# Sample attention's ScalarE and VectorE chains issued inside their own tick instead of behind the next main step

## What is computed

```python
def stick_breaking_attention(q, kc, vc, q_pos, bias):
    z = jnp.einsum('bqhd,bkhd->bhqk', q, kc) * (HEAD_DIM ** -0.5) + bias
    valid = jnp.arange(kc.shape[1])[None, :] < q_pos[:, None]
    log_beta = jnp.where(valid, jax.nn.log_sigmoid(z), -jnp.inf)
    log_keep = jnp.where(valid, jax.nn.log_sigmoid(-z), 0.0)
    later = lax.cumsum(log_keep, axis=3, reverse=True) - log_keep
    a = jnp.exp(log_beta + later)
    return jnp.einsum('bhqk,bkhd->bqhd', a, vc)
```

## Time and profile before

| | |
|---|---|
| median of 3 runs | 2498.41 us (2497.21 to 2503.57) |
| the profiled execution | 2500.48 us, of which span 2498.8 us |
| PE busy | 2340.1 us, 94% |
| DVE busy | 1191.4 us, 48% |
| ACT busy | 929.4 us, 37% |
| POOL busy | 142.2 us, 6% |
| PE waiting for `sa_kt` copies of ACT ahead of L2508, layer 0's mixers | 8.7 us in 5 waits |
| PE waiting for L1587 ahead of L1646, layer 0's mixers | 1.3 us in 2 waits |

### The profile page before, as it was taken

One profiled execution on the slowest core, in us unless ns is written; L12 is line 12 of the kernel. 1 busy time (PEld: TensorE's weight loads), 2 busy tenths in 40 slices (PEclk: granted clock), 3 DMA queues, 4 the chain that ended last, 5 costly groups with the idle time before them and its releaser, 6 DMA issues. The chain is left out here.

```text
span 2498.8 us, 44904 instructions
## 1 busy us (share of the span) xinstructions
PE 2340.1 (94%) x17622; PEld 2087.6 (84%) x17622; DVE 1191.4 (48%) x2080; ACT 929.4 (37%) x1671; POOL 142.2 (6%) x195
## 2 busy tenths in 40 slices
PE   7999999989988899999999999999798888999997
PEld 7999998766656599999899999987565566999996
DVE  6343273245566566342463434622656565643425
ACT  5222242223425554222352323321333365532333
POOL 0000010011222000000000000100112200000000
PEclk8999999989989799999999999999898897999998
DMA  5233333145756443233333233421558645333333
GB/s 141 68 84 84 102 112 125 51 126 165 228 163 184 144 144 88 67 90 84 96 86 84 78 91 102 129 91 34 185 176 227 195 128 178 85 85 84 82 102 91
DMA packets 384957, 290.97 MB, mean 116 GB/s; under 512 B 51808, under 2 KB 368392, under 8 KB 384272
## 3 DMA queue, kind: packets, MB, share of 16 engines
q1 hardware_dynamic: 368128, 234.08, 33.3%
q0 software_dynamic: 16128, 54.54, 7.1%
q10 hardware_dynamic: 528, 0.02, 0.0%
HBM read 274.99 MB, written 13.58 MB: 115 GB/s over the span
## 5 line engine op out<-in xcount | busy, mean ns | idle before, releaser
L218 PE MATMUL ps<-h_hi,w_hi 128*128 128x288 f32 x2400 | 719.1, 300 | 24.2 <-PEq L174 17.3
L219 PE MATMUL ps<-h_lo,w_hi 128*128 128x288 f32 x2400 | 711.2, 296 | 0.0
L220 PE MATMUL ps<-h_hi,w_lo 128*128 128x288 f32 x2400 | 710.6, 296 | 0.0
L242 DVE TENSOR_TENSOR w_lo<-w_raw,w_hi 128x2048 fp32r<-128x2048 f32 x145 | 332.3, 2291 | 341.2 <-ACT w_hi L236 341.1
L218 PEld LDWEIGHTS ps<-h_hi,w_hi 128*128 128x128 f32 x2400 | 453.1, 189 | 30.3 <-issue 25.2
L219 PEld LDWEIGHTS ps<-h_lo,w_hi 128*128 128x128 f32 x2400 | 453.3, 189 | 1.0
L220 PEld LDWEIGHTS ps<-h_hi,w_lo 128*128 128x128 f32 x2400 | 453.1, 189 | 0.0
L236 ACT ACTIVATE w_hi<-w_raw 128x2048 fp32r<-128x2048 f32 x145 | 276.7, 1908 | 163.9 <-PE ps L220 159.6
L218 PE MATMUL ps<-f_a_hi,w_hi 128*128 128x288 f32 x1024 | 302.7, 296 | 0.0
L220 PE MATMUL ps<-f_a_hi,w_lo 128*128 128x288 f32 x1024 | 301.6, 295 | 0.0
L219 PE MATMUL ps<-f_a_lo,w_hi 128*128 128x288 f32 x1024 | 301.5, 294 | 0.0
(11 more groups left out here) (345 smaller groups left out, 3167.9 us busy)
## 6 DMA issues: line engine op xcount, KB each, us to landing
w_raw<-in_w_ffn_in SPq DMA_DIRECT2D x132, 512.0 KB, 5.2
w_raw<-in_w_ffn_out SPq DMA_DIRECT2D x80, 512.0 KB, 4.9
sa_vn<-in_cache_sb_v SPq DMA_DIRECT2D x256, 128.0 KB
w_raw<-in_w_in SPq DMA_DIRECT2D x52, 512.0 KB, 4.6
sa_vn<-in_cache_win_v SPq DMA_DIRECT2D x96, 128.0 KB
w_raw<-in_w_out SPq DMA_DIRECT2D x24, 512.0 KB, 6.5
sa_kn_early<-in_cache_win_k POOLq DMA_DIRECT2D x72, 128.0 KB, 3.8
sa_vn<-in_cache_win_v SPq DMA_DIRECT2D x16, 512.0 KB
```

The costliest lines, as they stand in the source:

```text
L218: pe.matmul(out, stat_hi, mov_hi, start=start, stop=False, skip_group_check=True)
L219: pe.matmul(out, stat_hi, mov_lo, start=False, stop=False, skip_group_check=True)
L220: return pe.matmul(out, stat_lo, mov_hi, start=False, stop=stop, skip_group_check=True)
L242: dve.tensor_tensor(E["w_lo"][:, slot], E["w_raw"][:, slot], E["w_hi"][:, slot].bitcast(F32), ALU.subtract).then_inc(S["w_lo"], 1)
```

## The change

The content of `scalar_behind` and `vector_behind` moves into the tick's own functions, and `weave` loses its deferred call. ACT's tick is now: key copy; window exponential; the exponential of the chunk due one tick ago; the three-instruction ACT chain of the chunk due now; and only then the copy of turned weights and the gathered output copy. DVE's tick is: key copy; the DVE chain of the chunk due one tick ago; `take`; window reduce; weight copy; `rows`. No instruction is added or removed, no wait changes, and PE, SP and POOL are issued as before. Weights are still turned in tick T+3.

```diff
     def scalar_tick(act, t):
         if t < U:
             copy_keys_a(act, t)
-        for m in G["turn_at"].get(t, ()):
-            if m % 2 == 0:
-                copy_weights_a(act, chunks[m])
-        if t - 1 in G["ends"]:
...
-    def scalar_behind(act, t):
         for q in rows_at(t, 1):
             act.wait_ge(S["negated"], q["row"] + 1)
...
             act.activation(f_of(c), f_of(c), ACT.Exp, scale=-1.0).then_inc(S["exp_done"], 1)
             act.wait_ge(S["exp_done"], s + 1)
             act.activation(f_of(c), f_of(c), ACT.Ln, bias=1.0).then_inc(S["ln_done"], 1)
+        for m in G["turn_at"].get(t, ()):
+            if m % 2 == 0:
+                copy_weights_a(act, chunks[m])
+        if t - 1 in G["ends"]:
...
             spread_queries(dve, True)
         if t < U:
             copy_keys_b(dve, t)
+        for c in weighed_at(t, 1):
+            s, w = c["stick"], c["width"]
+            dve.wait_ge(S["ln_done"], s + 1)
+            dve.scalar_tensor_tensor(f_of(c), z_of(c), 0.0, f_of(c), ALU.max, ALU.add).then_inc(S["f_done"], 1)
...
+            dve.wait_ge(S["sum_done"], s + 1)
+            dve.tensor_tensor(z_of(c), z_of(c), f_of(c), ALU.subtract).then_inc(S["scanned"], 1)
         for c in chunks:
             if c["tick"] == t:
                 take(dve, c)
+        for q in rows_at(t, 0):
+            dve.wait_ge(S["z_ready"], q["chunk0"] + q["chunks"])
+            dve.tensor_reduce(mx[:, q["g"]:q["g"] + 1], zw[:, q["g"]], AX.X, ALU.max).then_inc(S["maxed"], 1)
...
         for m in G["turn_at"].get(t, ()):
             if m % 2 == 1:
                 copy_weights_b(dve, chunks[m])
-
-    def vector_behind(dve, t):
         if t in G["ends"]:
             p = G["ends"][t]
             q = passes[p]
...
-    def weave(eng, name, behind=None):
+    def weave(eng, name):
         mains = {tag: p[name](eng) for tag, p in parts.items()}
-        done, left = 0, None
+        done = 0
         for tag, upto in zip(ORDER, plan):
             next(mains[tag])
-            if left is not None:
-                behind(eng, left)
-                left = None
             while done < upto:
-                if left is not None:
-                    behind(eng, left)
                 side[name](eng, done)
-                left = done if behind else None
                 done += 1
```

More of the change, by code:

```diff
@@ L2664, in scalar_behind @@
             act.activation(f_of(c), f_of(c), ACT.Ln, bias=1.0).then_inc(S["ln_done"], 1)
+        for m in G["turn_at"].get(t, ()):
+            if m % 2 == 0:
+                copy_weights_a(act, chunks[m])
+        if t - 1 in G["ends"]:
+            p = G["ends"][t - 1]
+            q = passes[p]
+            chunk, at = (4 if q["window"] else 6), SEQ + SG * DEC_SEQ * q["g"]
+            e = ev_a["g", p]
+            act.wait_ge(S["turned_a"], e + 1)
+            act.activation(M["mixT"][:, chunk:chunk + 2, at:at + SG * DEC_SEQ],
+                           ps[:, TURN_A[e % len(TURN_A)], 0:64].rearrange("p (k t) -> p k t", k=2),
+                           ACT.Copy).then_inc(S["free_a"], 1)
     def spread_queries(dve, window):
@@ L2725, in vector_tick @@
             copy_keys_b(dve, t)
+        for c in weighed_at(t, 1):
+            s, w = c["stick"], c["width"]
+            dve.wait_ge(S["ln_done"], s + 1)
+            dve.scalar_tensor_tensor(f_of(c), z_of(c), 0.0, f_of(c), ALU.max, ALU.add).then_inc(S["f_done"], 1)
+            dve.wait_ge(S["f_done"], s + 1)
+            carried = 0.0 if c["first"] else f[:, (s - 1) % Z_SLOTS, 0:1]
+            dve.tensor_tensor_scan(f_of(c)[:, ::-1], one[:, 0:1].to_broadcast([P, w]), f_of(c)[:, ::-1], carried,
+                                   ALU.mult, ALU.add).then_inc(S["sum_done"], 1)
+            dve.wait_ge(S["sum_done"], s + 1)
+            dve.tensor_tensor(z_of(c), z_of(c), f_of(c), ALU.subtract).then_inc(S["scanned"], 1)
         for c in chunks:
@@ L2749, in vector_behind @@
                 dve.tensor_tensor(rows[:], ps[:, OUT_BANK, 0:W4], head_cols[:], ALU.mult).then_inc(S["rows_ready"], 1)
[L2750 to L2765, removed]
     sticks = [c for c in chunks if not c["window"]]
@@ L2772, in sample_attention @@
     return dict(S=S, zw=zw, spent=spent, ticks=G["ticks"], early_sync=early_sync, early_gpsimd=early_gpsimd,
-                keys=[landed(False, U - SLOTS + x) for x in range(SLOTS)], sync=sync_tick, gpsimd=gpsimd_tick, tensor=tensor_tick, scalar=scalar_tick, vector=vector_tick,
-                scalar_behind=scalar_behind, vector_behind=vector_behind)
+                keys=[landed(False, U - SLOTS + x) for x in range(SLOTS)], sync=sync_tick, gpsimd=gpsimd_tick, tensor=tensor_tick, scalar=scalar_tick, vector=vector_tick)
 TICK_RATE = dict(ml=0.565, ro=0.3, gl=0.43, pa=0.222)
@@ L2834, in _ @@
             act.preload_act_table_set(ROOT_TABLES)
-            weave(act, "scalar", side["scalar_behind"])
+            weave(act, "scalar")
         @block.vector
         def _(dve):
-            weave(dve, "vector", side["vector_behind"])
+            weave(dve, "vector")
 def output(nc, E, M, l, I, g_next, load_next):
```

5 lines of the change are left out of this document (3 added, 2 removed).

## The result

The changed kernel takes **2514.3 us** (median of 6 runs, 2508.0 to 2517.0) against 2497.8 (6 runs, 2491.1 to 2503.6). The ratio is **1.0062, with a 95% interval of 1.0042 to 1.0081**: slower, by the ratio about 15.5 us. The forecast was 2517, in a range of 2502 to 2537, with slower as the likeliest side. The profiled execution took 2514.6 us with a span of 2512.9, against 2500.5 and 2498.8 before: 14.1 us more.

The account below looks back on a forecast made before the run. PE's order was taken to set the length of the two mixers stages. Terms summed to +7.0 us per layer, +14.0 for both, plus +5 for the clock: +19 on 2498.4, so 2517 us, range 2502 to 2537.

Parts of the forecast that it names:

- 9 to 11: Tick 9: DVE's chain delays the main step's L1587, +1.2 us; a later 0.46 us wait goes; +0.7 net per layer.
- 28 to 33: Ticks 29 to 31: DVE's chain starts in a 1.25 us idle gap ahead of the rotary copies; -1.1 us per layer.
- The signs in the profile: Waits: L1646 5 us or more per layer, L2525 over 3, L2589 about 2.9; L2508's 4.84 falls by 2 or more.
- Ticks 13, 16 and 17: Chains ahead of L1587 (ticks 13, 16) and `take` (17) keep PE waiting: +1.9, +1.7 and +2.3 us per layer.
- Rival A: PE's work in ticks 9 to 18 covers the delays, so only gains stay: faster, down to 2487 us; chance 0.12.
- Ticks 5 to 7: Chain fits DVE's 3.30 us idle gap; later key copies come forward, shortening PE's 4.84 us wait: -2.7 us per layer.
- Tick 24: Weight and gather copies behind ACT's chain cost +2.1 us; tick 25's DVE chain in idle time gains -1.3; net +0.8 per layer.
- Tick 33: Chain ahead of L1868 costs +2.7 us but no longer stands between the next two GLA steps; +1.1 per layer.
- The window passes: Reduce and exponential ahead of prompt-attention steps, mostly covered by PE's prompt work: +2.3 us per layer, bounds 0 and 6.
- The clock: One new low-clock stretch per layer, near ticks 16 and 17, 2.7 us each: +5 us in all, between 0 and +16.
- Rival C: Clock and window passes reach their upper ends, mean clock in the windows below 0.87: +37 us, 2536; chance 0.12.
- The loads: Mixers stages: no PE wait names a DMA, so the key and value queues on POOL and SP only shift with PE.

Follow-up runs that it names:

- ACT's three alone: Kernel before, with only ACT's three-instruction chains (all but tick 17's) ahead of the next main step, weight and gather copies behind them: 1.0079.
- `take` ahead: Changed kernel with `take` put ahead of DVE's chain in each tick: 1.0042 against before, median 2507.0 us.
- chunk 4 alone: Kernel before, with only chunk 4's chains moved ahead, on both ACT and DVE: 0.9984, median 2496.4 us.
- the windows alone: Kernel before, with only the window passes' reduce and exponential and the `rows` steps ahead of the next main step: 0.9999.
- the single: Kernel before, with only DVE's chains of chunks 12 and 32 and their exponentials moved ahead: 1.0030, median 2506.4 us.
- the longer chain: Kernel before, with DVE's chains of chunks 12 and 32 ahead and four multiplications by 1.0 in front of chunk 12's: 1.0063, 2517.7 us.
- the sticks alone: Kernel before, with all the chunks' ACT and DVE chains ahead as in the changed kernel, window passes and `rows` left behind: 1.007.
- the weight copies in front: Changed kernel with ACT's weight and gathered output copies put back ahead of ACT's chain: 1.0045 against before, median 2510.0 us.
- DVE's chains alone: Kernel before, with only DVE's chains and their exponentials on ACT ahead of the next main step: 1.0026, 2507.3 us.

## Why the prediction was right, and where it was not

**The bound and the method** held. PE's order set the stage's length, and of the nine terms per layer four (9 to 11, 13, 16, 17) are within 0.4 us in both layers, two more (24 to 28, 28 to 33) within 0.7. The signs in the profile came as listed: L1646 at 5.3 us, L2525 over 3, L2589 at 3.1 for 2.9, the wait ahead of L2508 down from 4.84 to 0.95, ACT's idle time ahead of the exponential still there (3.29 us). Only the stages' lengths are short of what I wrote: 6.8 and 5.4 us more instead of 8 to 11, and 1.9 us came outside them, where I had written that nothing changes.

**Ticks 13, 16 and 17** are the core of the loss: +1.9, +1.7 and +2.3 forecast, 1.91, 1.69 and 2.02 measured. Rival A wanted cover in front of these waits; the arrivals show none. That the losses are these chains' and not something that the change does as a whole is shown by the kernels that hold only some of them: DVE's chain of chunk 12 (with chunk 32 far behind it) moves tick 14 and leaves 14 to 17 as before, ACT's three alone leave tick 13 to 14 as before and move 16 to 17, and `take` ahead of the chain takes back all of tick 17's.

**Ticks 5 to 7: right mechanism, over-sized.** I took -2.7 on the ground that DVE's later key copies come forward by that much. They did (tick 7 came 3.9 and 3.4 us sooner), but then L2557 waits 2.96 us for tick 7's key copy, and in layer 0 the main step's matmuls behind it took 1.92 us (L1648) and 1.68 (L1652) instead of 1.02 each at low clock; in layer 1 the steps of ticks 7 and 8 ran at 0.54 and 0.91. Net -1.7 and +0.4. With chunk 4 alone it was -4.0 and -2.0, so the term is between -4 and +0.4 by where the low stretches lie. -2.7 was inside, and one profile does not fix it better: against before, ticks 0 to 9 were between -1.8 and +1.7 us also in the three kernels in which no stick chain before tick 12 is moved (the windows alone, the single and the longer chain).

**Tick 24: right net, wrong reading of its parts.** PE's wait for the gather copy is 3.06 us as forecast (2.9), and L1278's fell from 2.20 to 0.48. But the wait brought low clock at once. In the eight layers with such a wait, 2.8 to 3.3 us (the changed kernel, the sticks alone, `take` ahead, ACT's three alone), the step at tick 25 ran at 0.50 to 0.62, and at 1.00 in before and in the kernel with the weight copies in front; it took 4.1 and 4.2 us in the changed kernel and 3.1 and 3.0 in the latter.

**Tick 33**: +1.1 forecast, +1.0 and +2.5. The chain moved PE's wait from L1972's second use to its first, and made it 2.68 us; the step in which it stands ran at 0.78 and 0.71.

**The window passes: wrong.** I took +2.3 per layer between 0 and 6. Alone they are 0 (-5.5 to +4.8 us for the kernel), and 0 was no lower bound: ticks 36 to the output stage came 4.1 us sooner in layer 1 of the changed kernel. I had written that PE's prompt work covers most of a reduce; it covers little, as PE's wait for L2191 grew by 1.35 us in the trace shown above. And I had not asked who waits for the exponential: it comes sooner and shortens PE's wait for it from 2.3 to 1.3 us. That was the one place where I did not go through the timeline.

**The clock: right in kind, wrong in place and price.** I took one new low stretch per layer, near ticks 16 and 17, at 2.7 us, +5 in all. In the changed kernel there is none there: the steps from 13, 16 and 17 ran at 1.00 in both layers, and PE's busy time in the stages fell by 4 us. Over all kernels with these waits (1.6 to 2.0 us at ticks 13 and 16, 3.1 at tick 17) a low stretch came behind 10 of 36, and cost 1.0 to 1.7 us each, not 2.7. Rival C, with a mean clock below 0.87, is out. The 2.7 came from a step with PE busy nearly throughout and a granted clock of 0.61; these ten had 0.83 or 0.84, so the lower level held for a smaller part of them. By the Trainium skill's "TensorE: Matmul & The Clock Gate" (section Terms) the penalty is half of the throttled time, which for steps of 10 us at 0.83 is an estimate of 1.7 us. Nine of the ten agree with it within 0.3 us; the tenth cost 1.0.

Where the low clock is new in the changed kernel is tick 25 and the step from tick 33, at the waits of 3.1 and 2.7 us. I had put nothing there. The second is in part moved and not added: before, it was the next step that ran at 0.70 and 0.82.

**The loads.** I had written that the DMA queues only shift with PE. That held for the changed kernel, which has no PE wait on a DMA. It did not hold where PE comes sooner: with the weight copies ahead PE waited up to 1.88 us for a load, and with `take` ahead 1.1 and 1.5 us per layer for values of the window passes.

**The total** was right partly by luck. The measured sticks contain what the clock did behind them, so they stand against sticks and clock together: forecast +14.4, measured alone about +17 (10 to 25 us). The windows were forecast at +4.6 and measured alone at 0 (-5.5 to +4.8). In the two traces the ledger's rows up to tick 36 sum to +14.8 for both layers. The places alone were forecast at 9.4, so they cost 5.4 more than I said, mostly at ticks 0 to 9 and 33 to 36 of layer 1, and a clock term of 5 that belonged elsewhere happens to cover it. The last row is -2.7 instead of +4.6. The traces thus show +12.1 in the stages where I had +19; that the times came out only 3 us below the forecast is more agreement than the terms have.

## What to carry to other kernels

When filler work is put ahead of a main engine's evictions, price it place by place: it gains only where the engine that runs it is idle in front of it and something that the bottleneck waits for stands behind it, and it loses where two main steps follow each other with nothing between. There the loss is its length less the slack that the eviction behind it had: at tick 13 the chain and its exponential are 3.3 us, ACT had been idle ahead of L1587, and 1.9 us were lost; of the 1.8 us by which the chain was then made longer, all were. Such an order should be chosen per place and not by one rule; here the chains of three chunks ahead made the kernel 0.6% faster, those of five others 0.7% slower, though only about half of the gain could be placed. PE that comes sooner can also meet a load that is not there yet. And read the granted clock of the step behind each wait that you make or remove, since it can double the worth of either.

## What the runs showed of the hardware

**The same wait lowers the clock or doesn't.** The granted clock knows two levels, 1.00 (2.4 GHz) and 0.50 (1.2 GHz). A wait of 1.85 us at tick 13 left it at full in 11 of 14 layers; one of 3.69 us lowered it in 2 of 2; 3.1 us at tick 17 lowered it in 4 of 10; 2.8 to 3.3 us at tick 24, between short groups, in 8 of 8. The length of the wait alone does not decide.

**The clock swings without a change.** The step from tick 41 took 7.2 us at 1.00 in layer 0 of before and 9.2 at 0.52 in layer 1, with the same work:

```profile
759.20:766.40 7.20, 5.79 (x52) 1.00 1.04 344
...
1985.20:1994.40 9.20, 8.97 (x51) 0.52 0.98 312
```

Some ten such steps would make a spread like that of the kernel before, 2485.8 to 2507.8 us in 27 runs; that they are its cause is not shown, as only one of its runs has a trace. A single profile's stretch is 2 us off by such a step alone: ticks 40 to 45 of layer 1 were 4.8 us shorter than before in the kernel with DVE's chains alone, which moves nothing there.

**A delay on VectorE of 0.4 and 1.0 us.** In the eight kernels from ACT's three alone onward, DVE starts `take` later behind the same matmuls than in the others: the stretch 11 to 13 is 0.4 us longer, and the one from 17 to 19 is 1.0 longer where it has nothing else new (PE waits 1.54 us for L2737 instead of 0.50), in both layers of every one, also where DVE's order is exactly that of before. These eight ran on other chips than the four kernels ahead of them, and the kernel before was 2500 us there instead of 2495.5; which chip the traces of the kernel before and the changed one are from is not on record. That the chip is the cause fits, but was not tested. The ratios are not touched by it, since before ran on the same chip. Arrivals of these eight kernels against before's trace contain it, 1.4 us per layer where nothing hides it.
